# A hybrid decoder layer on eight cores: seven of sixteen input tiles transposed by DMA, an earlier V load, a 16-column pooling edge, and new planner figures

## What is computed

```python
h = rms_norm(x, norm_mix)
q, k, v, u, g_a, g_p = split(h @ w_in)          # 512, 512, 512, 512, 1024, 1024
q, k = rope(rms_norm(q)), rope(rms_norm(k))     # 8 heads of 64, rotary on 16 dims
A = moba_attention(q, k, v)                     # own block of 256 causal + 3 best past blocks
B = multiscale_pool(u)                          # trailing means over 2/4/8/16 tokens, minus the token,
                                                # then a 128x128 linear per group and a scale
m = sigmoid(g_a) * (A @ w_up_attn) + sigmoid(g_p) * (B @ w_up_pool)
x = x + m @ w_out
x = x + relu(rms_norm(x) @ w_ff1)**2 @ w_ff2
```

## Time and profile before

| | us |
|---|---|
| median of 3 runs | 955.06 |
| the three runs | 953.29, 955.06, 1034.62 |
| the profiled execution, its own time | 950.71 |
| its span on the slowest core (core 7) | 949.6 |
| spans of the eight cores | 945.3 to 949.6 |
| TensorE busy, share of the span | 908.0, 96% |
| VectorE, ScalarE, GpSimd busy | 461.8, 375.2, 75.4 |

### The profile page before, as it was taken

The page is one execution under the profiler, slowest core; times in us unless marked ns, Lnnn a source line. Parts: engine busy times, 40 slices in busy tenths (PEclk is TensorE's granted clock), DMA queues, the critical chain, the costliest instruction groups (busy, mean ns, idle before and its releaser), DMA issues.

```text
span 949.6 us, 17253 instructions; the slowest of 8 cores (945.3 to 949.6 us)
## 1 busy us (share of the span) xinstructions
PE 908.0 (96%) x5772; PEld 466.0 (49%) x5772; DVE 461.8 (49%) x876; ACT 375.2 (40%) x738; POOL 75.4 (8%) x133
## 2 busy tenths in 40 slices
PE   2797999899999999999999999999999999999997
PEld 1354555566677764444444444444444444444443
DVE  2578877555533324344774444444444443444443
ACT  2566666698889872222005344031111221111120
POOL 4212110321000000100001000000000000000000
PEclk9899999999999999999999999999999999999999
DMA  8952034633433435892989804250064100002113
GB/s 187 212 131 68 2 76 89 83 52 69 68 68 57 78 68 117 166 207 73 211 133 158 120 1 62 40 78 1 1 89 64 27 1 1 1 0 80 59 62 156
DMA packets 57895, 76.31 MB, mean 80 GB/s; under 512 B 27792, under 2 KB 46224, under 8 KB 57552
## 3 DMA queue, kind: packets, MB, share of 16 engines
q0 software_dynamic: 24288, 40.28, 28.0%
q1 hardware_dynamic: 33520, 34.92, 13.4%
HBM read 98.41 MB, written 8.39 MB: 112 GB/s over the span
## 4 chain that ended last, share of the span: by engine, by line
PE 87%; DMA 6%; DVE 3%; issue 2%; ACT 1%; SPq 0%; POOL 0%; DVEq 0%; ACTq 0%; POOLq 0%
PE bank L1315 23%; PE bank L1341 23%; PE bank L988 10%; PE bank L429 8%; PE bank L882 6%; PE bank L1225 6%; PE bank L920 3%; PE bank L1002 3%; PE bank L1007 3%; DMA raw<-w_qkvu 3%; DMA raw<-x 2%; DMA raw<-w_slice 1%; PE bank L483 1%; DVE raw L399 0%; DMA raw<-raw 0%
## 5 line engine op out<-in xcount | busy, mean ns | idle before, releaser
L1322 ACT ACTIVATE raw<-bank 128x512 f32<-128x512 f32 x128 | 76.5, 598 | 376.5 <-PE bank L1315 317.9
L1315 PE MATMUL bank<-raw 128*128 128x512 bf16 x1024 | 224.0, 380 | 0.0
L1341 PE MATMUL bank<-raw 128*128 128x512 bf16 x1024 | 223.1, 379 | 0.0
L1315 PEld LDWEIGHTS bank<-raw 128*128 128x128 bf16 x1024 | 100.4, 98 | 121.5 <-issue 2.8
L1341 PEld LDWEIGHTS bank<-raw 128*128 128x128 bf16 x1024 | 100.2, 98 | 120.8
L1324 DVE SCALAR_TENSOR_TENSOR raw<-bank,raw 128x512 bf16<-128x512 f32 x128 | 88.6, 692 | 141.7 <-ACT raw L1322 141.7
L889 ACT ACTIVATE raw<-bank 128x512 bf16<-128x512 f32 (+1 forms) x288 | 146.2, 593 | 22.2 <-PE bank L920 20.3
L1347 DVE SCALAR_TENSOR_TENSOR raw<-bank,raw 128x512 f32<-128x512 f32 x128 | 96.1, 751 | 112.7 <-PE bank L1341 112.3
L429 PE MATMUL bank<-raw 128*128 128x512 bf16 x512 | 124.0, 392 | 12.0 <-DMA raw<-w_qkvu 6.7
L988 PE MATMUL bank<-raw 128*128 128x512 bf16 x512 | 122.5, 379 | 0.7 <-DMA raw<-w_slice 0.7
L882 PE MATMUL bank<-raw 128*128 128x256 bf16 x576 | 98.3, 266 | 2.0 <-ACT raw L889 1.5
(11 more groups left out here) (91 smaller groups left out, 597.1 us busy)
## 6 DMA issues: line engine op xcount, KB each, us to landing
raw<-x SPq DMA_DIRECT2D x32, 512.0 KB, 6.7
raw<-w_ff POOLq DMA_DIRECT2D x16, 1024.0 KB, 12.7
raw<-w_slice POOLq DMA_DIRECT2D x22, 640.0 KB, 7.9
out<-raw SPq DMA_DIRECT2D x16, 512.0 KB, 2.7
raw<-w_qkvu POOLq DMA_DIRECT2D x8, 512.0 KB, 13.7
raw<-raw SPq DMA_DIRECT2D x2, 1024.0 KB, 6.9
raw<-w_out POOLq DMA_DIRECT2D x4, 512.0 KB, 13.2
raw<-c_ind POOLq DMA_DIRECT2D x4, 256.0 KB, 5.8
```

The costliest lines, as they stand in the source:

```text
L1315: t.group("pe", [lambda e, c=c, j=j, bk=bk: e.matmul(bank_f(bk), lhsT=ffw1[s][:, c, j * 128:(j + 1) * 128], rhs=hT[:, c, tg * 512:(tg + 1) ...
L1322: t.op("act", lambda e, bk=bk, si_=si_: e.activation(out=sqz[si_], in_=bank_f(bk), func=AF.Square), reads=hb[bk], writes=[b_sqz[si_]])
L1341: t.group("pe", [lambda e, j=j, bk=bk, hf=hf, i=i: e.matmul(bank_f(bk), lhsT=a1T[ab][:, j, i * 128:(i + 1) * 128], rhs=ffw2[s][:, j, hf * ...
```

## The change

- x tiles 9 to 15 (NT_PE = 9) are no longer transposed by TensorE and evicted: SP asks for a DMA transpose from hb0 into hT. hb0 gets a third buffer.
- The V weights wait for x slot 1, not slot 2.
- The planner gets other figures: arrival of the weights (W_AT) and of x (X_AT), an x load that holds SP for 2.6 instead of 0.45 us with a latency of 1.5 instead of 3.5 us, a `lag` (a piece's result is ready that much after its engine is free): 2.4 us for the DMA transposes, 8.5 us for the two kT2 copies.
- The tile-before matmul of band_mm writes 16 columns, not 128.
- The indicator DMAs are pieces of their own (load_ind), planned after the copy's lag.
- Band, band eviction, q transpose and q eviction pieces planned later than T_ATT - 4.0 are planned 1.2 us later.
- The last output tile is computed in pieces of 512, 256 and 256 columns, each with its own store.

```diff
--- before.py
+++ after.py
@@ -264,7 +264,7 @@
 
         junk = view(E0, [128, D], BF16)
         gmix_bc = view(E0 + 2 * KB, [128, D], F32)
-        hb0 = [view(E0 + 6 * KB + i * 2 * KB, [128, D], BF16) for i in range(2)]
+        hb0 = [view(o_, [128, D], BF16) for o_ in (E0 + 6 * KB, E0 + 8 * KB, G0 + 3584)]
         sq_sb = [view(E0 + 10 * KB + i * 2 * KB, [128, 512], F32) for i in range(2)]
         qtok = [view(E0 + (14 + i) * KB, [128, 512], BF16) for i in range(3)]
         x16 = [view(E0 + 17 * KB + i * 512, [128, 8, 16], F32) for i in range(2)]
@@ -314,7 +314,7 @@
         b_rstd1 = [Buf("rstd1_%d" % i) for i in range(NT)]
         b_junk = Buf("junk")
         b_hT = [Buf("hT_%d" % i) for i in range(NT)]
-        b_hb0 = [Buf("hb0_%d" % i) for i in range(2)]
+        b_hb0 = [Buf("hb0_%d" % i) for i in range(3)]
         b_sq = [Buf("sq%d" % i) for i in range(2)]
         b_x16 = [Buf("x16%d" % i) for i in range(2)]
         b_qtok = [Buf("qtok%d" % i) for i in range(3)]
@@ -408,6 +408,10 @@
                 identity=ident_b) for c in range(8)],
                 reads=[b_hb0[s2], b_ident], writes=hb[bk])
 
+        def p0_trd(tt, s2):
+            t.dma("sp", hT[:, :, tt * 128:(tt + 1) * 128], hb0[s2],
+                  reads=[b_hb0[s2]], writes=[b_hT[tt]], transpose=True)
+
         def p0_ev(eng, tt, bk):
             evict(eng, hT[:, :, tt * 128:(tt + 1) * 128], bank_bf(bk).rearrange("p (c t) -> p c t", c=8),
                   hb[bk], [b_hT[tt]])
@@ -515,12 +519,12 @@
                 kind = 2 if tt == 0 else 0
                 fns.append(lambda e, g=g, kind=kind: e.matmul(
                     bank_f(tbk)[:, g * 128:(g + 1) * 128], lhsT=u_sb[tt % NU][:, g * 128:(g + 1) * 128],
-                    rhs=band[:, g * 3 + kind, :], start=True, stop=(tt == 0)))
+                    rhs=band[:, g * 3 + kind, :], start=True, stop=True))
                 if tt > 0:
                     fns.append(lambda e, g=g: e.matmul(
-                        bank_f(tbk)[:, g * 128:(g + 1) * 128],
+                        bank_f(tbk)[:, g * 128:g * 128 + 16],
                         lhsT=u_sb[(tt - 1) % NU][:, g * 128:(g + 1) * 128],
-                        rhs=band[:, g * 3 + 1, :], start=False, stop=True))
+                        rhs=band[:, g * 3 + 1, 0:16], start=False, stop=True, skip_group_check=True))
             rd = [b_u[tt % NU], b_band] + ([b_u[(tt - 1) % NU]] if tt > 0 else [])
             t.group("pe", fns, reads=rd, writes=hb[tbk])
 
@@ -544,6 +548,9 @@
             b_kT2h[hf].fence = {"pe": t.cnt["pe"]}
             p0_, p1_ = 2 * hf, 2 * hf + 2
             t.dma("sp", kT2[:, p0_:p1_, :], kT[:, p0_:p1_, :], reads=b_kT, writes=[b_kT2h[hf]])
+
+        def load_ind(hf):
+            p0_, p1_ = 2 * hf, 2 * hf + 2
             for j in range(2):
                 b_ind[hf][j].fence = {b_kT2h[hf].w[0]: b_kT2h[hf].w[1]}
             ind_r = c_ind_d[p0_:p1_].rearrange("a r s -> r a s")
@@ -589,7 +596,7 @@
 
 
         class Task:
-            __slots__ = ("name", "prio", "opts", "deps", "get", "put", "slots", "start", "end", "eng", "after", "only")
+            __slots__ = ("name", "prio", "opts", "deps", "get", "put", "slots", "start", "end", "eng", "after", "only", "lag")
 
             def __init__(self, name, prio, opts, deps=(), get=(), put=(), after=0.0):
                 self.name, self.prio, self.opts = name, prio, opts
@@ -598,6 +605,7 @@
                 self.start = self.end = self.eng = None
                 self.after = after
                 self.only = None
+                self.lag = 0.0
 
             def emit(self):
                 for e_, _, fn in self.opts:
@@ -611,7 +619,7 @@
             tasks.append(k_)
             return k_
 
-        pools = {"x": list(range(NXS)), "hb0": [0, 1], "tp": [0, 1, 2], "pj": list(pj_banks), "sq": [0, 1],
+        pools = {"x": list(range(NXS)), "hb0": [0, 1, 2], "tp": [0, 1, 2], "pj": list(pj_banks), "sq": [0, 1],
                  "st": [0, 1, 2, 3], "x16": [0, 1], "qtok": [0, 1, 2], "u": list(range(NU)), "mb": [3]}
 
         def first_loads():
@@ -629,7 +637,7 @@
             t.dma("sp", gv_qk, c_gv_d.partition_broadcast(128), writes=[b_gv])
             t.dma("sp", rope_t, c_rope_d.rearrange("p (t n) -> p t n", t=NT), writes=[b_rope])
             p0_load(3)
-            t.wait_written("pool", b_xslot[2])
+            t.wait_written("pool", b_xslot[1])
             load_w(CG_V)
 
         first_loads()
@@ -638,28 +646,36 @@
             t.wait_written("pool", b_xslot[sl])
             load_w(cg)
 
-        W_AT = {CG_K: 14.5, CG_V: 26.0, CG_Q: 37.0, CG_U: 48.0}
-        X_AT = [4.5, 15.0, 16.5, 20.0]
+        W_AT = {CG_K: 15.0, CG_V: 30.0, CG_Q: 43.0, CG_U: 54.0}
+        X_AT = [4.7, 16.3, 18.6, 23.0]
         ji_of = {jb: ji for ji, jb in enumerate(jobs)}
         k_ev_t, q_ev_t, hev, ujob = {}, {}, {}, {}
+        NT_PE = 9
         x_ld = [None] * NT
         muls = [None] * NT
         prev_ld = None
         for tt in range(NT):
             pk = ji_of[(CG_K, tt)]
             if tt >= NXS:
-                x_ld[tt] = add("xld", pk - 9, [("sp", 0.45, lambda tt=tt: p0_load(tt))],
+                x_ld[tt] = add("xld", pk - 9, [("sp", 2.6, lambda tt=tt: p0_load(tt))],
                                deps=[muls[tt - NXS]] + ([prev_ld] if prev_ld else []))
                 prev_ld = x_ld[tt]
             arrive = X_AT[tt] if tt < NXS else 0.0
             sq_ = add("xsq", pk - 4.5, [("act", 1.55, lambda tt=tt: p0_sq(tt))],
                       deps=[x_ld[tt]] if x_ld[tt] else [], after=arrive)
             if x_ld[tt]:
-                sq_.after = -3.5
+                sq_.after = -1.5
             mul = Task("mul", pk - 3.5, [], deps=[sq_], get=["hb0"])
             mul.opts = [("dve", 1.45, lambda tt=tt, k_=mul: p0_mul(tt, k_.slots["hb0"]))]
             tasks.append(mul)
             muls[tt] = mul
+            if tt >= NT_PE:
+                tr = Task("trd", pk - 2.5, [], deps=[mul], put=[(mul, "hb0")])
+                tr.opts = [("sp", 0.9, lambda tt=tt, m_=mul: p0_trd(tt, m_.slots["hb0"]))]
+                tr.lag = 2.4
+                tasks.append(tr)
+                hev[tt] = tr
+                continue
             tr = Task("tr", pk - 2.5, [], deps=[mul], get=["tp"], put=[(mul, "hb0")])
             tr.opts = [("pe", 0.47, lambda tt=tt, k_=tr, m_=mul: p0_tr(tt, m_.slots["hb0"], k_.slots["tp"]))]
             tasks.append(tr)
@@ -738,7 +754,11 @@
         for g_ in range(4):
             add("wgs", 30.0 + 3 * g_, [("dve", 0.35, lambda g_=g_: scale_wg(g_))], after=85.0 + 8 * g_)
         kt2_0 = add("kt2a", 0.0, [("sp", 0.5, lambda: make_kT2(0))], deps=list(k_ev_t.values()))
-        add("kt2b", 0.0, [("sp", 0.5, lambda: make_kT2(1))], deps=[kt2_0, by_job[(CG_V, NT - 1)]])
+        kt2_0.lag = 8.5
+        kt2_1 = add("kt2b", 0.0, [("sp", 0.5, lambda: make_kT2(1))], deps=[kt2_0, by_job[(CG_V, NT - 1)]])
+        kt2_1.lag = 8.5
+        add("ind0", 60.0, [("pool", 2.0, lambda: load_ind(0))], deps=[kt2_0])
+        add("ind1", 60.0, [("pool", 2.0, lambda: load_ind(1))], deps=[kt2_1])
         km = add("kmean", 45.0, [("dve", 0.6, kmean_fin)], deps=list(k_ev_t.values()))
         for k_ in tasks:
             if "mb" in k_.get:
@@ -747,7 +767,7 @@
 
         LAT = 0.2
         free_at = {n_: {i: 0.0 for i in v_} for n_, v_ in pools.items()}
-        eng_free = {"pe": 0.0, "act": 0.0, "dve": 0.0, "pool": 22.0, "sp": 20.0}
+        eng_free = {"pe": 0.0, "act": 0.0, "dve": 0.0, "pool": 20.0, "sp": 22.0}
         INF = 1e18
         left = list(tasks)
         order = []
@@ -777,8 +797,9 @@
             pick = min(cand, key=lambda b_: (b_[2].prio, b_[1]))
             alt = min((b_ for b_ in best if b_[2] is pick[2]), key=lambda b_: (b_[1] + 0.02 * eng_free[b_[3]]))
             st_, en_, k_, e_ = alt
+            eng_free[e_] = en_
+            en_ += k_.lag
             k_.start, k_.end, k_.eng = st_, en_, e_
-            eng_free[e_] = en_
             for n_ in k_.get:
                 i_ = min((q_ for q_ in free_at[n_] if not k_.only or q_ in k_.only), key=lambda q_: free_at[n_][q_])
                 k_.slots[n_] = i_
@@ -792,6 +813,10 @@
         todo = sorted(order, key=lambda k_: (k_.start, seq[id(k_)]))
         T_ATT = last_root.end + LAT
         STEP_US = 0.85
+        for k_ in todo:
+            if k_.start > T_ATT - 4.0 and k_.name in ("band", "bev", "qtr", "qev"):
+                k_.start += 1.2
+        todo.sort(key=lambda k_: (k_.start, seq[id(k_)]))
         while todo and todo[0].start <= T_ATT - STEP_US:
             todo.pop(0).emit()
 
@@ -1335,20 +1360,25 @@
             s = fq % 2
             for i in range(4):
                 tt = tg * 4 + i
-                for hf in range(2):
+                final = fq == 3 and (tg, i) == (0, 3)
+                for c0_, c1_ in ((0, 512), (512, 768), (768, 1024)) if final else ((0, 512), (512, 1024)):
                     bk = f2_banks[f2_i % 4]
                     f2_i += 1
```

(22 more changed lines are left out.)

## The result

| | before | changed |
|---|---|---|
| undisturbed executions, us | 953.29, 954.17, 955.06 | 943.73, 943.86 |
| profiled execution, us | 950.71 | 943.86 |
| spans of cores 0 to 3 | 948.1, 948.2, 949.3, 946.5 | 941.3, 942.5, 936.7, 937.3 |
| spans of cores 4 to 7 | 946.9, 945.3, 947.2, 949.6 | 936.6, 934.2, 933.8, 937.4 |

The ratio of changed to before is 0.9891, 95% interval 0.9863 to 0.992: 10.4 us faster, and by the bound of 2% no difference. (Two more executions of the changed kernel had a die at a lower clock; they make its plain median 973.49 and are left out, as is the one of before.) The forecast was 943 us.

What follows compares the result with a forecast made beforehand. TensorE work plus 41.6 us idle, bound early by DMA, then VectorE and ScalarE queues, then full TensorE. Terms 6.1 + 3.15 - 1.0 + 1.8 + 0.7 + 1.0 = 11.75, say 12: 955.06 to 943 us; 8 in 10 within 935 to 952.

Steps and rivals of the forecast that it cites:

- V sooner: Early part: V weights asked for after x slot 1, at about 18.2 instead of 20.86 us, gain 2.7 us.
- there is room: DMA share 0.58 in 18 to 21 us leaves bandwidth for the earlier V load; 2.7 us, bound 0 if full.
- The new arrivals: Early part: planner's later V arrival puts tile 3's K job ahead of tile 0's V job, gain 3.4 us.
- now it believes 30: Planner's V arrival moves from 26 to 30 us, so tile 3's K job goes ahead of V; 3.4 us.
- Transposes by DMA: Tiles 9 to 15: 56 TensorE matmuls removed, landing in 3 to 4 us without waits, gain 3.15 us.
- the prediction's own last sentence: Landings above 5 us, TensorE waiting for DMA transposes, or attention under 5 us sooner would make the prediction wrong.
- VectorE in 70 to 110: VectorE, 87% busy at 70 to 110 us, gives early gain back: net loss 1.0 us.
- The bound of a gain of 4: Upper bound for the VectorE term in 70 to 110 us; its other bound was a loss of 6.
- The pooling edge: 60 pooling matmuls narrowed to 16 columns, each 0.030 us shorter, gain 1.8 us.
- Late consumers: At 177.51 us a pooling matmul's 1.54 us wait shrinks with the 1.2 us set-back; gain 0.7, bounds 0 and 1.5.
- The end: After the last matmul: shorter scale-and-add gains 0.3 us, smaller store 0.7, together 1.0 us.
- both limits fall: Rival: 70 to 110 us idle goes nearly whole, early part gives 8; gain 19.6 us, 935 us, chance 0.09.

Runs made afterwards that it cites:

- e2: Changed kernel, but the V weights wait for x slot 2 again; ratio to before 0.9874.
- e4: Changed kernel with the old assumed arrivals of weights and x (W_AT, X_AT) put back; ratio to before 0.9959.
- e8: Kernel before with only the new assumed arrivals (W_AT, X_AT); ratio to before 1.0022.
- e10: Changed kernel with the planner's old free times put back (POOL free at 22, SP at 20); ratio to before 0.9866.
- e3: Changed kernel with NT_PE = 16, all 16 tiles transposed by TensorE and none by DMA; ratio to before 0.9934.
- e12: Kernel before with only the 16-column pooling edge and the last tile in three pieces; ratio to before 0.9961.
- e1: Changed kernel without the 1.2 us set-back of the late band and q pieces; ratio to before 0.9875.
- e11: Changed kernel, with all pieces planned later than 0.3 us before attention's start moved 0.86 us, replacing the 1.2 us set-back; ratio to before 0.9853.
- e6: Changed kernel, but rotary steps of q jobs among the last four jobs are offered only to VectorE; ratio to before 0.9902.
- e7: Changed kernel with late q rotary steps offered only to VectorE and without the 1.2 us set-back; ratio to before 0.9892.
- e9: Kernel before with the planner's new arrivals, x-load cost and POOL and SP free times (20 and 22); ratio to before 0.9983.

## Why the prediction was right

The time was right (943 forecast, 943.8 measured; 12 us forecast, 10.4 and 12.4 measured on two chips). Its terms were right in two cases of seven, and the errors cancelled: that the sum came out is luck. Point by point:

- **V sooner, 2.7 us: wrong, worth 0.** The step that failed is "there is room". The share of 0.58 in 18 to 21 was read on the core with the latest V load, and what counts is when the second half lands, behind a full DMA. e2.
- **The new arrivals, 3.4 us: the swap came, but not by the arrivals, and the size and the place were wrong.** The K job does go ahead of V, and the two run at full clock. The step that failed is "now it believes 30, so the K job of tile 3, planned ready at about 28, goes ahead of V": with V believed at 26 it goes ahead too (e4), and with 30 it stays behind where POOL and SP have their old free times (e8, e10). Those two numbers, which the prediction doesn't name, set the first jobs; in the changed kernel they are worth 4.7 us of idle time in the first 50 us (e10). Against before the first 50 us gain only 1.8, since other waits grew. What the arrivals do in the changed kernel lies later: 4.4 us idle between 50 us and attention with them, 14.1 without (e4). I priced one swap of two jobs, where the figures set the order of all.
- **Transposes by DMA, 3.15 us: right** on TensorE's side (3.2 us in attention's start, e3). Landing took 3.1 to 5.0 us on core 7 (median 3.5, taken 3 to 4), 3.0 to 5.6 on all eight. TensorE waited for two of them, 0.6 us on core 7. By the prediction's own last sentence, landings above 5 us or such waits would make it wrong; both came, at a price of 0.6 us. The time moves by some 6 us in e3, so the term was rather too small.
- **VectorE in 70 to 110, a loss of 1.0 us: wrong in sign.** What I read as a limit of VectorE (87% busy) was an order that didn't fit the chip. VectorE is still at 85% there (33.82 of 40), and TensorE's idle time is down from 6.4 to 2.2 us. VectorE's relief is worth 0.4 to 1.1 us between 50 us and attention (e3), the order the rest. The bound of a gain of 4 was passed.
- **The pooling edge, 1.8 us: right.** 60 x 0.030 us, e12 and the rows above.
- **Late consumers, 0.7 us: wrong in sign.** The set-back itself is worth nothing (e1). But the stretch behind attention's start lost 4.3 us, which goes with the planned order there and the clock that falls with it. I had said that the trace of before can't show the new order, and kept that doubt to VectorE's stretch alone.
- **The end, 1.0 us: too small, 1.8 us** (5.2 to 3.4). Scale-and-add 0.48 us as taken; the store 1.8 against 2.7 us; the last matmul is itself half as long (256 columns, 0.107 us less). Another 0.4 us lies between the store's landing and the end of the span (core 7: 1.07 us before, 0.63 now), where no term looked.

Sum of the terms as measured: 0 + 1.8 + 3.2 + 6.9 + 1.8 - 4.3 + 1.8 = 11.2 us, against 11.75 forecast and 10.4 and 12.4 measured. The rival "both limits fall" came true in its first half, and the loss at attention's start, for which I had no rival, held it back to the forecast.

What stays open: what lowers the idle time between 50 us and attention in e10 without the two free times, and which of the pieces makes the 4.3 us behind attention's start. The two planned shapes separate all kernels but e11, the rotary isn't it (e6), the set-back isn't it (e1, e7), and the shift gives back half. The 2 us that e3 loses behind attention's start have no row either.

## What to carry to other kernels

Where engines work queues that a planner wrote, an engine at 85 to 90% beside a waiting TensorE isn't yet a limit: look whether the planned times of arrival are those of the trace, and change all of them together, since one figure alone can bring nothing (e8) and its removal cost 8 us (e4). Look at the numbers that nobody named as well: two start times of idle engines decided the first jobs (e10), and whether 20 and 22 are nearer to the trace than 22 and 20 no run shows. Before a gain is put down to a figure, take that figure alone back and see whether the order it is said to make is gone: here it wasn't (e4). Time won ahead of a seam between two stages has to be followed across the seam: e9 started attention 7.7 us sooner and kept 1.6 (interval -0.9 to 4.1). And read the time at which a transfer is asked for on all cores, and price it by when it lands.

## What the runs showed of the hardware

- Behind a matmul of 16 columns with its own weight load the next starts after 0.026 us (0.025 behind one of 2 or 8 columns), behind one of 128 after 0.056 us.
- DMA transposes of a 128x1024 bf16 tile, asked for one at a time beside single x loads, landed in 3.0 to 5.6 us (median 3.2, eight cores), 1.2 us of it the issue. The SP queue holds 7,680 packets more than before (33,520 to 41,200), of which the two further stores of the last tile are a part; packets under 512 B are 7,424 more (27,792 to 35,216).
- Four waits of 0.9 to 1.6 us in the 20 us from attention's start were followed by 3.4 or 6.8 us at 1.2 GHz on five of eight cores, and on the other three, with the same waits, by none. Before, with fewer waits there (0.7 and 1.7 us on every core), one core fell, at the end of a further wait of 2.1 us.
- The granted clock doesn't show all the time at half rate: in the changed kernel (core 7) eight matmuls of 512 columns from 23.70 us on, behind waits of 4.50 and 1.26 us, stood 0.42 us apart, at a granted clock of 1.00 in 23 to 27 us.
